# Row scaling of the attention weights on GpSimd, in a two-block transformer kernel on one core

## The reference, cut to what matters

```python
# block 1, 8 heads of 64 (forgetting_attention)
p = softmax(q @ k.T * scale + gate_sums, causal)     # rows sum to 1
fox_out = (p @ v) * silu(fg)                         # fg: a gate of 512 x 512

# block 2, 16 heads of 64, 4 groups of keys and values (swa_sink_attention)
m = maximum(max(scores), sink)
e = exp(scores - m)
probs = e / (sum(e) + exp(sink - m))
out = (probs @ v) @ w_o + b_o
```

## Time and profile before

| | us |
|---|---|
| runs of the kernel before (3) | 1484.49, 1484.64, 1486.16; median 1484.64 |
| profiled execution: span from first to last instruction | 1484.1 |
| PE busy in the span | 1475.0 (99%) |
| POOL busy | 902.7 (61%) |
| DVE busy | 708.6 (48%) |
| ACT busy | 435.8 (29%) |
| first attention | about 142 to 192 in the span |
| second attention | about 957 to 1029 |

### The profile page before, as it was taken

The page is one execution under the profiler, slowest core; times in us unless marked ns, Lnnn a source line. Parts: engine busy times, 40 slices in busy tenths (PEclk is TensorE's granted clock), DMA queues, the critical chain, the costliest instruction groups (busy, mean ns, idle before and its releaser), DMA issues.

```text
span 1484.1 us, 19739 instructions
## 1 busy us (share of the span) xinstructions
PE 1475.0 (99%) x7150; PEld 1199.4 (81%) x7150; DVE 708.6 (48%) x863; ACT 435.8 (29%) x884; POOL 902.7 (61%) x719
## 2 busy tenths in 40 slices
PE   9999999999999999999999999999999999999999
PEld 7888677888888888888888888867888888888887
DVE  5674658350046676003541284877777300552253
ACT  3242665141123422001210053766152100221032
POOL 7766035486633597666776656810659666777653
PEclk9999999999999999999999999999999999999999
DMA  6323011233311233332333322400323333233322
GB/s 208 110 89 101 22 44 57 85 100 99 99 58 56 86 108 105 99 99 89 96 99 99 99 71 86 128 30 15 100 72 113 100 99 98 89 97 99 99 85 86
DMA packets 37315, 132.72 MB, mean 89 GB/s; under 512 B 4304, under 2 KB 4736, under 8 KB 37248
## 3 DMA queue, kind: packets, MB, share of 16 engines
q1 hardware_dynamic: 36576, 129.52, 28.2%
q10 hardware_dynamic: 672, 2.23, 0.4%
HBM read 129.59 MB, written 2.10 MB: 89 GB/s over the span
## 4 chain that ended last, share of the span: by engine, by line
PE 97%; ACT 2%; DVE 1%; DMA 0%; issue 0%; SPq 0%; ACTq 0%
PE PS L644 22%; PE PS L645 22%; PE PS L646 22%; PE PS L595 3%; PE PS L596 3%; PE PS L577 3%; PE PS L826 2%; PE PS L669 1%; PE PS L670 1%; PE PS L671 1%; PE PS L1105 1%; PE PS L918 1%; PE PS L933 1%; PE PS L790 1%; PE PS L788 1%; PE PS L789 1%
## 5 line engine op out<-in xcount | busy, mean ns | idle before, releaser
L536 POOL TENSOR_TENSOR W_lo<-W_raw,W_hi 128x1024 fp32r<-128x1024 f32 x238 | 600.5, 2523 | 19.9
L533 POOL TENSOR_TENSOR HOLD<-HOLD 1x1 f32<-1x1 f32 x238 | 63.5, 267 | 544.9 <-PE PS L646 302.4
L644 PE MATMUL PS<-A_hi,W_hi 128*128 128x512 f32 x904 | 352.3, 390 | 0.1
L646 PE MATMUL PS<-A_lo,W_hi 128*128 128x512 f32 x904 | 351.8, 389 | 0.0
L645 PE MATMUL PS<-A_hi,W_lo 128*128 128x512 f32 x904 | 351.7, 389 | 0.0
L534 POOL TENSOR_SCALAR W_hi<-W_raw 128x1024 fp32r<-128x1024 f32 x238 | 247.4, 1040 | 0.0
L644 PEld LDWEIGHTS PS<-A_hi,W_hi 128*128 128x128 f32 x904 | 169.7, 188 | 36.9 <-issue 0.8
L644 PE MATMUL PS<-H_hi,W_hi 128*128 128x512 f32 x512 | 199.2, 389 | 0.0
L645 PE MATMUL PS<-H_hi,W_lo 128*128 128x512 f32 x512 | 199.2, 389 | 0.0
L646 PE MATMUL PS<-H_lo,W_hi 128*128 128x512 f32 x512 | 199.2, 389 | 0.0
L646 PEld LDWEIGHTS PS<-A_lo,W_hi 128*128 128x128 f32 x904 | 169.7, 188 | 35.3
(11 more groups left out here) (346 smaller groups left out, 2045.7 us busy)
## 6 DMA issues: line engine op xcount, KB each, us to landing
W_raw<-in_weights SPq DMA_DIRECT2D x238, 512.0 KB, 3.5
X<-in_x SPq DMA_DIRECT2D x4, 512.0 KB, 7.3
out<-X SPq DMA_DIRECT2D x7, 256.0 KB, 4.2
RELU<-in_ple_in ACTq DMA_DIRECT2D x2, 512.0 KB, 3.6
CONST<-in_constants ACTq DMA_DIRECT2D x1, 849.5 KB, 6.5
PARAM<-in_params SPq DMA_DIRECT2D x1, 320.5 KB, 8.8
SIN<-in_positions ACTq DMA_DIRECT2D x1, 256.0 KB, 3.8
out<-X SPq DMA_DIRECT2D x2, 128.0 KB, 1.7
```

What stands on the lines that cost most here:

```text
L533: pool.tensor_tensor(HOLD[:, 1 + s:2 + s], HOLD[:, 0:1], HOLD[:, 0:1], ALU.add)
L536: pool.tensor_tensor(W_lo[:, s, :], W_raw[:, r, :], W_hi[:, s, :].bitcast(F32), ALU.subtract).then_inc(w_lo, 1)
L644: pe.matmul(PS[:, bank, :], W_hi[:, slot, w], hi[:, kk, :], start=first, stop=False)
L646: done = pe.matmul(PS[:, bank, :], W_hi[:, slot, w], lo[:, kk, :], start=False, stop=last)
```

## The change

The rows of P are divided before they are transposed, by a new piece of work on POOL. It scales each piece of `PR` in place by its row's inverse sum. With that the whole spreading goes: ACT's widening, PE's four transposes a pair, DVE's product with or copy of the share. Inverses are taken by group, not by pair. Output banks alternate between 0 and 1 (`out_bank`), so a pair's first weigh waits for the mix of the pair before the last. `PR` grows from two to four slots (first attention), so ACT may run two groups ahead. PE's order in a group becomes scores(g+2), weigh(g-1), transposes(g). In the second attention ACT takes `A_hi`, and DVE `A_lo`, straight from the output bank.

```diff
+            def scale(rows, column):
+                return pool.tensor_scalar(rows, rows, column, None, ALU.mult)
+            def fox_shares():
+                for g in range(FOX.steps):
+                    pool.wait_ge(FOX.inverted, g + 1)
+                    for h in range(2):
+                        for first, i, width in fox_blocks(g):
+                            at = FOX.column(i, h)
+                            last = scale(PR[:, fox_slot(g, h), first:first + width], sum_columns(g // 3)[:, at:at + 1])
+                        last.then_inc(FOX.scaled, 1)
+            def window_shares():
+                for v in range(SWA.steps):
+                    p, i, width = v // NT, v % NT, SWA.width(v)
+                    if v % 2 == 0:
+                        pool.wait_ge(SWA.inverted, v // 2 + 1)
+                    for h in range(2):
+                        at = SWA.column(i, h)
+                        last = scale(PR3[:, v % 4, h * width:h * width + width], sum_columns(p)[:, at:at + 1])
+                    last.then_inc(SWA.scaled, 1)
+            splits(0, W_SLOTS)
+            splits(W_SLOTS, PLAN["late1"].first + 3)
+            fox_shares()
+            splits(PLAN["late1"].first + 3, PLAN["out3"].first + 2)
+            window_shares()
+            splits(PLAN["out3"].first + 2, N_BLOCKS)
...
 # PE, first attention
-                    pe.wait_ge(FOX.exped, 2 * g + h + 1)
+                    pe.wait_ge(FOX.scaled, 2 * g + h + 1)
...
-                    if g % 3 == 0 and p:
-                        pe.wait_ge(mix_ready, KD + p)
+                    if g % 3 == 0 and p >= 2:
+                        pe.wait_ge(mix_ready, KD + p - 1)
...
                 for g in range(FOX.steps):
+                    if g + 2 < FOX.steps:
+                        scores(g + 2)
                     if g == FOX.steps - 1:
-                        pe.wait_ge(FOX.exped, 2 * g)
-                        late_tile(1, 2, range(0, 2))
+                        late_tile(1, 2, range(1, 2))
+                    if g:
+                        weigh(g - 1)
+                    if g == FOX.steps - 2:
+                        pe.wait_ge(FOX.exped, 2 * (g + 1))
+                        late_tile(1, 2, range(0, 1))
                     transposes(g, 0)
                     transposes(g, 1)
-                    if g:
-                        weigh(g - 1)
-                        if g % 3 == 0:
-                            spread_inverse(FOX, g // 3 - 1)
-                    if g + 2 < FOX.steps:
-                        scores(g + 2)
...
 # PE, second attention
-                    pe.wait_ge(SWA.exped, 2 * v + 2)
+                    pe.wait_ge(SWA.scaled, v + 1)
...
-                    transposes(2 * g)
-                    if g == 0:
-                        scores(2)
-                    transposes(2 * g + 1)
+                    if g + 2 < 2 * SWA.pairs:
+                        scores(g + 2)
                     if g:
                         weigh(2 * g - 2)
                         weigh(2 * g - 1)
-                        if g % 2 == 0:
-                            spread_inverse(SWA, g // 2 - 1)
-                    if 0 < g < 2 * SWA.pairs - 2:
-                        scores(g + 2)
+                    transposes(2 * g)
+                    transposes(2 * g + 1)
...
 # DVE, first attention
+                maxima(0)
+                maxima(1)
                 for g in range(FOX.steps):
+                    inverse(g)
+                    if g + 2 < FOX.steps:
+                        maxima(g + 2)
+                    copy(g)
+                    if g % 3 == 0 and g:
+                        mix(g // 3 - 1)
...
 # DVE, second attention
+                def low(p):
+                    low_part(p, stage_at, PS[:, out_bank(p), :])
...
+                    inverse(g)
+                    if g + 2 < 2 * SWA.pairs:
+                        maxima(g + 2)
+                        sinks(g + 2)
+                    copy(2 * g + 1)
                     if c == 0 and p:
-                        inverse(p - 1)
...
+                        low(p - 1)
+                low(SWA.pairs - 1)
```

More of the change, by code:

```diff
@@ L537, in split, with splits @@
                                    ALU.subtract).then_inc(w_lo, 1)
+            def splits(first, last):
+                uses = W_SLOTS // RAW_SLOTS
+                whole, end = -(-first // W_SLOTS), last // W_SLOTS
+                for n in range(first, min(last, whole * W_SLOTS)):
+                    split(n, n % W_SLOTS, n // RAW_SLOTS)
+                if whole < end:
+                    with pool.Fori(whole, end) as g:
+                        for s in range(W_SLOTS):
+                            split(g * W_SLOTS + s, s, g * uses + s // RAW_SLOTS)
+                for n in range(max(first, end * W_SLOTS), last):
+                    split(n, n % W_SLOTS, n // RAW_SLOTS)
@@ L1913, in copy, with inverse @@
                     dve.tensor_copy(PT[:, 2 * (g % 2) + 1, 0:width], PS[:, 7, 0:width]).then_inc(FOX.read_by_dve, 1)
-                def inverse(p):
-                    dve.wait_ge(FOX.exped, 2 * 3 * (p + 1))
-                    dve.reciprocal(sum_columns(p), sum_columns(p)).then_inc(FOX.inverted, 1)
+                def inverse(g):
+                    blocks = fox_blocks(g)
+                    at = FOX.column(blocks[0][1], 0)
+                    columns = sum_columns(g // 3)[:, at:at + 2 * len(blocks)]
+                    dve.wait_ge(FOX.exped, 2 * (g + 1))
+                    dve.reciprocal(columns, columns).then_inc(FOX.inverted, 1)
                 def mix(p):
-                    dve.wait_ge(FOX.spread, p + 1)
-                    dve.tensor_tensor(SHARE[:], PS[:, SPREAD_BANK, :], G1[:, p, :], ALU.mult).then_inc(FOX.shared, 1)
-                    dve.wait_ge(FOX.shared, p + 1)
                     dve.wait_ge(FOX.weighed, 3 * (p + 1))
-                    dve.tensor_tensor(mixed1(p), PS[:, O_BANK, :], SHARE[:], ALU.mult).then_inc(mix_ready, 1)
+                    dve.tensor_tensor(mixed1(p), PS[:, out_bank(p), :], G1[:, p, :], ALU.mult).then_inc(mix_ready, 1)
+                maxima(0)
+                maxima(1)
                 for g in range(FOX.steps):
-                    p, c = g // 3, g % 3
-                    maxima(g)
-                    if g:
-                        copy(g - 1)
-                    if c == 0 and p:
-                        inverse(p - 1)
-                    if c == 1 and p:
-                        mix(p - 1)
-                copy(FOX.steps - 1)
-                inverse(FOX.pairs - 1)
+                    inverse(g)
[4 more added lines that the diff above has]
+                        mix(g // 3 - 1)
                 mix(FOX.pairs - 1)
@@ L1996, in window_attention @@
                     p, c = g // 2, g % 2
-                    if g >= 2:
-                        maxima(g)
-                    if c:
-                        sinks(p)
-                    if g:
-                        copy(2 * g - 1)
-                    if c == 0 and p:
-                        inverse(p - 1)
-                    if c and p:
-                        mix(p - 1)
-                    if c == 0 and p >= 2:
-                        low_part(p - 2, stage_at, MIX[:, 0, :])
-                copy(SWA.steps - 1)
-                inverse(SWA.pairs - 1)
-                low_part(SWA.pairs - 2, stage_at, MIX[:, 0, :])
-                mix(SWA.pairs - 1)
-                low_part(SWA.pairs - 1, stage_at, MIX[:, 0, :])
+                    inverse(g)
[3 more added lines that the diff above has]
+                    copy(2 * g + 1)
+                    if c == 0 and p:
+                        low(p - 1)
+                low(SWA.pairs - 1)
             def pool(c):
```

139 lines of the change are left out of this document (52 added, 87 removed).

## The result

The changed kernel takes **1535.04 us** (median of four runs, 1534.20 to 1537.78) against 1484.64: a ratio of 1.0339, 95% interval 1.0327 to 1.0352, so it is slower by 3.4%. The forecast was 1488.3 us with a range up to 1504.0. Its sign was right, its size was not, and the time lies outside the range.

A forecast was written before the change was run, and what follows sets the result against it. TensorE was taken to bound both attentions, nearly always busy. The second attention's +4.4 us and the first's -0.7 us gave +3.7 us, added to the median 1484.64: 1488.3 us, range 1481.5 to 1504.

The forecast's parts named there:

- the price of one scaling: POOL's multiplication of a piece by its inverse sums: 0.40 us for 256 columns, 0.61 for 512.
- the line: POOL price through the `W_hi` row and a 1x1 row: 0.18 us plus 0.84 ns a column.
- rival 1: Scaling costs more by column, 1.5 ns, so both attentions wait: together +18 us, 1502.6 us; chance 0.30.
- The chain: Between transposes of successive groups: copy, sometimes `A_lo`, addition, inverse, two scalings; second attention +4.4 us in all.
- The wait into groups with 256 columns: Second attention, six groups with `A_lo` in the way: TensorE waits 0.8 us each, 4.9 us together.
- The start: Second attention: first inverse stands behind the second copy of V; waits of 0.7 and 0.6, 1.3 us.
- The end: Second attention: no scores left as cover for the last groups and last weigh; 4.1 us together.
- the gain by what leaves TensorE's list: Second attention: eight spreads gone, 3.9 us, and the old order's waits gone, 2.5 us.
- The spreads: First attention: four spreading transposes of 0.59 us leave TensorE, a gain of 2.4 us.
- The wait of weigh(9): Near the first attention's end, it directly follows its transposes and waits for DVE's copy, 0.8 us.
- Alternating banks: Output banks in turn: no weigh waited for a mix before, so no effect was counted.
- the upper line: Upper bound from POOL's two-input `W_lo` row: 0.73 us for 256 columns, 1.27 for 512, some +35 us.

The follow-up runs named there:

- Experiments 1 to 3: Changed kernel, GpSimd scaling by two constants, two operations: 1485.85 us; by column and constant, two operations: 1493.1 us; by one constant, one operation: 1528.04 us.
- Experiment 1: Changed kernel with each GpSimd scaling multiplying by two constants 1.0 instead of the column, division left out: 1485.85 us, ratio 1.0006.
- experiment 5: Changed kernel with two-operation scaling (column, then 1.0) and VectorE's inverse of the next group moved ahead of the copy: 1480.26 us, ratio 0.9966.
- Experiment 6: Changed kernel with its one-operation scaling kept and only VectorE's inverse moved ahead of the copy: 1492.73 us.
- experiment 8: Against experiment 5's kernel: TensorE's first-attention order back to transposes, weigh, scores, with scores three groups ahead of the transposes behind them: 1478.83 us, ratio 0.9960.

## Why the prediction was wrong

**The step that failed** is the price of one scaling, 0.40 us for 256 columns, where 0.93 us was measured: "I take the line, for the scaling has one tensor input". The line went through `W_hi`. That instruction has one tensor input too, but the code beside the row shows another form: it multiplies twice by 1.0, while the scaling multiplies once and has no second operation. Experiments 1 to 3 show that just this decides. Counting inputs was the wrong likeness; the form of the instruction, number of operations included, was the right one, and no instruction of that form stood in POOL's list before.

**The bound was too narrow.** As the upper end stood the nearest two-input row, 0.73 us for 256 columns and "some +35". The instruction took 0.93 us, and the kernel lost 50. And the range left even this bound out, since rival 1 was priced at 1.5 ns a column, a value between the lines that no row had. By the bounds of its own table the range would have reached to 1520, and would still have missed. Beside it, the Trainium skill (GPSIMD Engine Reference, 3.1 Elementwise) gives 769 ns as the best case for 512 elements; here it was 619 to 695 ns with two operations and 1491 to 1565 with one, so neither agrees.

**Rival 1 named the mechanism.** "The scaling costs more by column" happened, at more than its price. Its signs were those seen: rows of 0.56 us and more, transposes that wait for POOL, up to 1.9 us.

**The chain was right, its terms were too high.** Experiment 1 is the prediction at its own price. Second attention: +4.4 us forecast, +0.7 measured. The wait into groups with 256 columns, forecast 0.8 us, was 0.6 (a pair takes 7.03 us there and 6.44 in experiment 5). The start (0.7 and 0.6 forecast) had waits of 0.41 and 0.30. The end, priced at 4.1 us, shows 2.2: 0.17, 0.27, 0.30, 0.41, and 1.08 into the last group where 2.0 was forecast. And the gain by what leaves TensorE's list was larger: a pair fell from 7.35 to 6.44 in experiment 5, 0.91 us, where 0.49 of the spread and 0.23 of the wait were counted. Of the other 0.19, 0.10 is in the eight transposes: 1.02 us ahead of a weigh, 0.92 ahead of the masks (990.11 to 991.03 in experiment 5). The first attention and the stretch between were 0.7 and 0.9 us worse than forecast, so the total of experiment 1 comes nearer to 1488.3 than its parts do.

**First attention: a missing term.** The spreads were to give 2.4 us, and the stage stayed at 50.0 in experiments 1 and 5. The sum took PE's pieces at their old lengths in a new order. In the new order they are longer. A pair took 9.55 us before, from the spread at 159.98 to the next one:

```profile
169.53 0.66 PE L817 MATMUL PS<-CONST,TO_TURN 128*128 128x128 f32 x4
```

Without its spread that would be 9.55 - 0.59 = 8.96 us. In experiment 5 it is 9.35, 1.2 us more in three pairs:

```profile
158.56 1.09 PE L856 MATMUL PS<-PT,V 128*64 128x128 f32 x16
...
167.91 1.09 PE L856 MATMUL PS<-PT,V 128*64 128x128 f32 x16
```

The wait of weigh(9), forecast 0.8, is there with 0.7, though for ScalarE's copy and not for VectorE's (experiment 5):

```profile
179.84 0.88 PE L856 MATMUL PS<-PT,V 128*64 128x128 f32 x12 [0.70 <-ACT PT L1399]
```

**What was hidden stayed hidden.** Alternating banks and the late splits of the weights appear among no waits of note; one of 0.5 us of PE for `W_lo` is in the profile after (0.9 in experiment 5), at a place outside both attentions that the prediction did not look at. Between the attentions all variants take 765.7 to 767.1 us, before 765.1; what these 1 to 2 us are was not settled. The experiment without scalings has them too (766.8).

**The shared way to memory** cost nothing that can be seen. The inverses of four columns in the second attention take 179 ns on average in the profile after and in experiment 1 alike, and the negated maxima 222 and 256 ns where they took 214 before.

**The dependence on the price was right.** From its own sum (+3.7 us at 0.40 us) to the upper line (+35 at 0.73) the prediction has 95 us for each us of a 256-column scaling. Measured, from experiment 1 to the changed kernel, it is 49.2 us for 0.518, the same 95. By this rate (an estimate) the right price would have brought the sum to some 1538 us. So the price alone took the time out of the range, and the chain that it was put into was the right one. A chain without slack passes on every nanosecond of its links: the second attention did with the column's 4.8 us, while the first, which had slack, passed on 0.5 of 2.4.

## What to carry to other kernels

Price a new instruction by one of the same form: engine, operation, number of operations and kinds of operands, and treat a likeness in inputs alone as no evidence. On GpSimd, give a `tensor_scalar` of this kind (float32, from SBUF to SBUF) a second, neutral operation. And before a link of a chain is made faster, look whether it can start earlier: taking the inverse ahead of the copy was worth as much (42 us) as the threefold cheaper instruction, and only both together made the change a gain.

## What was unexpected of the hardware

- One operation costs GpSimd three times as much a column as two: 2.5 against 0.83 ns, with 0.2 to 0.3 us fixed. That holds for a constant and for a column of scalars.
- TensorE's clock fell behind some of the waits, and the work after them paid for it. In the profile after, the granted clock is 0.88 on average in the second attention. In these two stretches TensorE first waits at a clock that is still mostly full, then is busy throughout at 0.50, the lower of the two levels:

```profile
992.00:994.00 2.00, 0.63 (x4) 0.45 (x3) 0.33 (x2) 1.08 (x5) 1.50 (x2) 0.90 0.05 8
994.00:996.00 2.00, 2.00 (x8) 1.04 (x8) 0.94 (x3) 1.12 (x5) 0.23 (x1) 0.50 0.00 0
```

  It is at 0.50 again from 1079.36 to 1082.30, when TensorE is already without waits in `out3` (busy 2.94 of 2.94 us). The rest of the span is 1.5 us longer than before, which is about what three microseconds at half clock cost. Not every wait does it: from 1034 to 1050 TensorE is busy 10.66 of 16 us, and the clock stays at 1.00. Experiment 6, with fewer waits and the same instruction, shows a mean clock of 1.000 and the rest at 455.2 us.
- The order of kinds of products on TensorE has a price that shows as no wait: 2.04 or 1.90 us for the same three pieces (experiment 8). Why was not settled.
